# Value products of the sink attention as three rounded products, in one layer of a streaming encoder

## What is computed

```python
s = jnp.einsum("bnqhgd,bnkhd->bnhgqk", q, k) * ATTN_SCALE
s = jnp.where(mask, s, -jnp.inf)
m = jnp.maximum(jnp.max(s, axis=-1, keepdims=True), sink)
e = jnp.exp(s - m)
p = e / (jnp.sum(e, axis=-1, keepdims=True) + jnp.exp(sink - m))
return jnp.einsum("bnhgqk,bnkhd->bnqhgd", p, v)        # the value product
```

## Time and profile before

| | us |
|---|---|
| median of 3 runs (lowest, highest) | 2725.19 (2724.36, 2726.61) |
| the profiled execution: its time | 2727.1 |
| its span, first to last instruction | 2725.5 |
| TensorE busy with matmuls in the span | 2649.0 (97%) |
| VectorE, ScalarE, GpSimd busy | 1814.1, 1267.0, 459.6 |

### The profile page before, as it was taken

How to read it: one execution, slowest core, us unless ns; L and a number is a source line. 1 busy time by engine, 2 the same in 40 slices (tenths; PEclk the granted TensorE clock), 3 DMA queues, 4 the chain that set the end, 5 groups by cost and what they waited for, 6 DMA issues and landing times.

```text
span 2725.5 us, 50555 instructions
## 1 busy us (share of the span) xinstructions
PE 2649.0 (97%) x19461; PEld 2566.0 (94%) x19461; DVE 1814.1 (67%) x2898; ACT 1267.0 (46%) x2367; POOL 459.6 (17%) x726
## 2 busy tenths in 40 slices
PE   7899999999989989999999999899999999999998
PEld 6787899999979989999999999899999999999998
DVE  7754434343464457688888888788888888877632
ACT  5444434433442225566666666554445455525421
POOL 0110012111221111133333333220111010000000
PEclk9999999999999999999999999999999999999999
DMA  4111122222212225355555555875554563422331
GB/s 157 59 47 39 36 86 83 80 76 80 77 43 78 79 72 182 133 187 187 185 190 192 193 189 193 300 264 181 215 215 134 174 215 108 136 88 78 107 100 58
DMA packets 108283, 360.77 MB, mean 132 GB/s; under 512 B 17696, under 2 KB 25760, under 8 KB 107552
## 3 DMA queue, kind: packets, MB, share of 16 engines
q1 hardware_dynamic: 66880, 224.29, 25.4%
q0 software_dynamic: 39568, 132.23, 13.1%
q10 hardware_dynamic: 1616, 1.18, 0.1%
HBM read 282.59 MB, written 75.04 MB: 131 GB/s over the span
## 4 chain that ended last, share of the span: by engine, by line
PE 92%; DVE 3%; DMA 3%; ACT 1%; issue 1%; ACTq 0%; DVEq 0%; POOL 0%; POOLq 0%
PE tile L614 33%; PE misc L696 18%; PE misc L978 16%; PE tile L696 5%; PE tile L978 4%; PE tile L666 4%; PE misc L807 4%; PE misc L614 3%; DMA a_raw<-in_w 2%; PE misc L787 1%; PE misc L709 1%; PE misc L755 1%; PE misc L754 1%; DVE stat L1565 1%; DMA acc<-h_saved_d 0%
## 5 line engine op out<-in xcount | busy, mean ns | idle before, releaser
L614 PE MATMUL tile<-x_hi,w_hi 128*128 128x288 f32 (+1 forms) x2208 | 498.9, 308 | 17.2 <-DVE x_lo L1542 7.9
L614 PE MATMUL tile<-x_hi,w_lo 128*128 128x288 f32 (+1 forms) x2208 | 476.2, 298 | 0.0
L614 PE MATMUL tile<-x_lo,w_hi 128*128 128x288 f32 (+1 forms) x2208 | 475.8, 297 | 0.0
L614 PEld LDWEIGHTS tile<-x_hi,w_hi 128*128 128x128 f32 (+1 forms) x2208 | 352.6, 189 | 44.5 <-issue 36.3
L614 PEld LDWEIGHTS tile<-x_hi,w_lo 128*128 128x128 f32 (+1 forms) x2208 | 356.8, 189 | 1.3
L614 PEld LDWEIGHTS tile<-x_lo,w_hi 128*128 128x128 f32 (+1 forms) x2208 | 356.7, 189 | 1.2
L1017 ACT ACTIVATE a_lo<-a_raw 128x512 fp32r<-128x512 f32 (+1 forms) x420 | 274.0, 656 | 175.7 <-PE misc L978 88.9
L1472 DVE TENSOR_TENSOR w_lo<-w_raw,w_hi 128x1024 fp32r<-128x1024 f32 x170 | 223.7, 1330 | 151.1 <-ACT w_hi L1017 151.0
L696 PE MATMUL misc<-t_hi,a_lo 128*128 128x288 f32 x1008 | 256.0, 294 | 0.0
L1017 ACT ACTIVATE w_hi<-w_raw 128x1024 fp32r<-128x1024 f32 x170 | 177.2, 1052 | 161.9 <-PE tile L614 126.0
L1898 DVE TENSOR_TENSOR a_lo<-a_raw,a_lo 128x512 fp32r<-128x512 f32 x336 | 221.2, 686 | 0.7 <-ACT a_lo L1017 0.7
(11 more groups left out here) (301 smaller groups left out, 5963.4 us busy)
## 6 DMA issues: line engine op xcount, KB each, us to landing
a_raw<-in_w SPq DMA_DIRECT2D x224, 512.0 KB, 4.1
w_raw<-in_w SPq DMA_DIRECT2D x170, 512.0 KB, 3.6
ops_d<-st POOLq DMA_DIRECT2D x280, 144.0 KB, 3.7
ops_d<-hr POOLq DMA_DIRECT2D x112, 144.0 KB, 4.5
x_hi<-ops_d POOLq DMA_DIRECT2D x24, 576.0 KB, 6.9
x_lo<-ops_d POOLq DMA_DIRECT2D x24, 576.0 KB, 10.1
t_hi<-ops_d POOLq DMA_DIRECT2D x24, 576.0 KB, 12.7
a_lo<-ops_d POOLq DMA_DIRECT2D x9, 576.0 KB, 11.5
```

Source lines behind the costliest of these rows:

```text
L614: ins = nc.tensor.matmul(dst[:, h, :], w, x[:, h * HALF:(h + 1) * HALF], start=first and a == 0, stop=last and a == 2)
```

## The change

The value product of the sink pairs becomes three fp32r products. The values are split into `sv` (rounded) and `sv_lo`, with a plane of 128 columns for each head that is zero in the other head's 64; the turned probabilities are split into `s_pt` and `s_pt_lo`, the latter a new VectorE subtraction in every slot from 3 to 12, on which the next transposes and the product wait (`turn_lo`). The weight splits of these tiles move from steps 0 and 8 to steps 1 and 3 (ScalarE) and 2 and 4 (VectorE). Plain float32 matmuls whose result nobody reads are put in the two idle stretches (`fill`). The new buffers take the place of the norm's scratch `st`.

```diff
+ACT_SPLITS, DVE_SPLITS = (1, 3), (2, 4)
...
@@ TensorE
-                    pe.wait_ge(turn_out, lin(g0 + s + 1, i, dg))
+                    pe.wait_ge(turn_lo if kind == "swa" else turn_out, lin(g0 + s + 1, i, dg))
...
-                    pe.wait_ge(turn_out, lin(g0 + s + 2, i, dg))
+                    pe.wait_ge(turn_lo if kind == "swa" else turn_out, lin(g0 + s + 2, i, dg))
...
+                    if kind == "swa":
+                        dst = out_ps[:, 128 * qt:128 * qt + 128] if qt < 4 else scores_ps[:, 512 - SAMPLE:512]
+                        n = 0
+                        for v, p_ in ((sv, s_pt), (sv_lo, s_pt), (sv, s_pt_lo)):
+                            for k, (vt, at) in enumerate(vals):
...
+                                ins = nc.tensor.matmul(dst, v[0:keys, at, head, :], p_[0:keys, s % 2, width * k:width * k + width],
...
+            def fill(count):
+                for k in range(count):
+                    nc.tensor.matmul(tiles_ps[0][:, 0, 0:128], mean_w[:, :], mean_w[:, :], start=True, stop=True)
...
             first_sums()
+            fill(29)
...
             ln_sums(1)
-
+            wait_freed(pe, T_MLP - 2)
+            wait_freed(pe, T_MLP - 1)
+            fill(31)
@@ ScalarE
-            copy(sv[:, 0:4, :], scores_ps[:, 0:512].rearrange("p (a b) -> p a b", a=4)).then_inc(sv_ready, 1)
-            copy(sv[0:64, 4, :], scores_ps[0:64, 512:640]).then_inc(sv_ready, 1)
-            act.wait_ge(sv_ready, 2)
+            for h in range(2):
...
+                copy(sv[:, 0:4, h, own], turned_values[:, :, own]).then_inc(sv_ready, 1)
+                copy(sv[0:64, 4, h, own], scores_ps[0:64, 512 + 64 * h:576 + 64 * h]).then_inc(sv_ready, 1)
+                copy(sv[:, 5, h, own], cv_raw[:, own]).then_inc(sv_ready, 1)
+            act.wait_ge(sv_ready, 6)
+            act.wait_ge(sv_lo_done, 6)
             set_sinks(0)
...
@@ ScalarE and VectorE (DVE_SPLITS there)
             def swa_pair(q, att, i=None, dp=0):
                 for c in range(KT):
-                    if c % 8 == 0:
-                        ahead.upto(U_QA + 2 * q + c // 8 + 2, i, 2 * dp)
                     swa_part(c, att, i, dp)
+                    if c in ACT_SPLITS:
+                        ahead.upto(U_QA + 2 * q + ACT_SPLITS.index(c) + 2, i, 2 * dp)
                     if q == 1:
                         gates(c)
@@ VectorE
+                if kind == "swa" and 3 <= j <= STEPS + 2:
+                    s = j - 3
+                    width = turn_width(kind, step_of(s)[1])
+                    dve.wait_ge(turn_out, lin(g0 + s + 2, i, dg))
+                    V.tensor_tensor(s_pt_lo[:, s % 2, 0:width], turn_ps[:, 0:width], s_pt[:, s % 2, 0:width], ALU.subtract)\
+                        .then_inc(turn_lo, 1)
...
+            dve.wait_ge(sv_ready, 6)
+            for h in range(2):
...
+                V.tensor_tensor(sv_lo[:, 0:4, h, own], turned_values[:, :, own], sv[:, 0:4, h, own], ALU.subtract).then_inc(sv_lo_done, 1)
+                V.tensor_tensor(sv_lo[0:64, 4, h, own], scores_ps[0:64, 512 + 64 * h:576 + 64 * h], sv[0:64, 4, h, own], ALU.subtract)\
+                    .then_inc(sv_lo_done, 1)
+                V.tensor_tensor(sv_lo[:, 5, h, own], cv_raw[:, own], sv[:, 5, h, own], ALU.subtract).then_inc(sv_lo_done, 1)
@@ GpSimd
-            for k, z in enumerate((sk2[64:128, 0, :].bitcast(f32), sk2[0:64, 1, :].bitcast(f32))):
+            for k, z in enumerate((sk2[64:128, 0, :].bitcast(f32), sk2[0:64, 1, :].bitcast(f32),
+                                   sv[:, :, 0, 64:128].bitcast(f32), sv[:, :, 1, 0:64].bitcast(f32))):
...
             pool.wait_ge(x_ready, 2 + KT)
+            for k, z in enumerate((sv_lo[:, :, 0, 64:128].bitcast(f32), sv_lo[:, :, 1, 0:64].bitcast(f32))):
+                P.memset(z, 0.0).then_inc(zeroed_p, 1)
```

More of the change, by code:

```diff
@@ L252, in build @@
         swa = ExitStack()
-        win_r = sb("win_r", [128, 256], f32r, swa)
         sinks = sb("sinks", [128, 2 * PAIRS], f32, swa)
@@ L257, in build @@
         sq1 = sb("sq1", [128, 2, TOK], f32r, swa)
-        sv = sb("sv", [128, 6, 128], f32, swa)
+        sv = sb("sv", [128, 6, 2, 128], f32r, swa)
+        cv_raw = sb("cv_raw", [128, 128], f32, swa)
         s_p = sb("s_p", [128, 4, 2 * 128 + 1], f32, swa)
-        s_pt = sb("s_pt", [128, 2, 256], f32, swa)
         cos_t = sb("cos_t", [128, TOK], f32, swa)
@@ L309, in build @@
         staged = (st[:, 0, :], st[:, 1, :])
+        st_flat = st_r[:, :, :].rearrange("p a b -> p (a b)")
+        sv_lo = st_flat[:, 0:1536].rearrange("p (a h b) -> p a h b", a=6, h=2)
+        s_pt = st_flat[:, 1536:2048].rearrange("p (a b) -> p a b", a=2)
+        s_pt_lo = st_flat[:, 2048:2560].rearrange("p (a b) -> p a b", a=2)
+        win_r = st_flat[:, 2560:2816]
         ops_d = nc.dram_tensor("ops_d", (JOBS, 2, FAST, 128, HALF), f32, kind="Internal").ap()
@@ L348, in build @@
         op_act, op_dve, op_pool = sem("op_act"), sem("op_dve"), sem("op_pool")
-        va_ready, va_turned, sv_ready = sem("va_ready"), sem("va_turned"), sem("sv_ready")
+        va_turned, sv_ready = sem("va_turned"), sem("sv_ready")
         kv_out = sem("kv_out")
@@ L361, in build @@
         turn_out = sem("turn_out")
+        turn_lo, sv_lo_done = sem("turn_lo"), sem("sv_lo_done")
         weighed = sem("weighed")
         out_free = sem("out_free")
-        v_ready, v_turned, fv_ready = sem("v_ready"), sem("v_turned"), sem("fv_ready")
-        k_ready = sem("k_ready")
+        v_turned, fv_ready = sem("v_turned"), sem("fv_ready")
         v_out, k_out, forget_rows = sem("v_out"), sem("k_out"), sem("forget_rows")
@@ L383, in build @@
         y_sum, y_ready = sem("y_sum"), sem("y_ready")
-        p_landed, p_hi_done, p_ready, pe_ready = sem("p_landed"), sem("p_hi_done"), sem("p_ready"), sem("pe_ready")
-        gate, gated = sem("gate"), sem("gated")
+        p_landed, p_hi_done, p_ready = sem("p_landed"), sem("p_hi_done"), sem("p_ready")
+        gated = sem("gated")
         y_out = [sem("y_out0"), sem("y_out1")]
-        ch_act, ch_dve, ch_pool = sem("ch_act"), sem("ch_dve"), sem("ch_pool")
+        ch_dve, ch_pool = sem("ch_dve"), sem("ch_pool")
         OP_KV = 4
@@ L491, in build @@
         block = outer.enter_context(nc.Block())
-        ZERO_SWA, ZERO_ALL = 2, 2 + 6
+        ZERO_SWA, ZERO_ALL = 6, 6 + 6
         f_tmp = acc[0:16, :, :].rearrange("p k t -> p (k t)")
@@ L782, in attend @@
                     pe.wait_ge(normed, lin(g0 + s + 1, i, dg))
-                    pe.wait_ge(turn_out, lin(g0 + s + 1, i, dg))
+                    pe.wait_ge(turn_lo if kind == "swa" else turn_out, lin(g0 + s + 1, i, dg))
+                    if kind == "fox" and pair == PAIRS and s == 0:
+                        pe.wait_ge(turn_lo, STEPS * PAIRS + 1)
                     cols_ = key_cols(kind, head, qt)
@@ L804, in attend @@
                     vals = value_tiles(kind, qt)
+                    if kind == "swa":
[3 more added lines that the diff above has]
+                            for k, (vt, at) in enumerate(vals):
+                                keys = SAMPLE if qt == 4 and k == len(vals) - 1 else 128
+                                n += 1
+                                ins = nc.tensor.matmul(dst, v[0:keys, at, head, :], p_[0:keys, s % 2, width * k:width * k + width],
+                                                       start=s in (0, 8) and n == 1, stop=n == 3 * len(vals),
+                                                       skip_group_check=s not in (0, 8))
+                        ins.then_inc(weighed, 1)
+                        return
                     for k, (vt, at) in enumerate(vals):
@@ L864, in swa_keys_ready @@
                 pe.wait_ge(zeroed_p, ZERO_SWA)
-                pe.wait_ge(sv_ready, 2)
+                pe.wait_ge(sv_ready, 6)
+                pe.wait_ge(sv_lo_done, 6)
                 pe.wait_ge(masks, 3)
@@ L1100, in _ @@
                 act.dma_start(dst[:, :], t[name]).then_inc(consts, 16)
-            act.dma_start(sv[:, 5, :], t["swa_cv"]).then_inc(consts, 16)
+            act.dma_start(cv_raw[:, :], t["swa_cv"]).then_inc(consts, 16)
             for c in range(KT):
@@ L1128, in _ @@
             act.wait_ge(va_turned, 1)
-            copy(sv[:, 0:4, :], scores_ps[:, 0:512].rearrange("p (a b) -> p a b", a=4)).then_inc(sv_ready, 1)
-            copy(sv[0:64, 4, :], scores_ps[0:64, 512:640]).then_inc(sv_ready, 1)
-            act.wait_ge(sv_ready, 2)
+            act.wait_ge(zeroed_p, 4)
+            for h in range(2):
+                own = slice(64 * h, 64 * h + 64)
+                turned_values = scores_ps[:, 0:512].rearrange("p (a b) -> p a b", a=4)
+                copy(sv[:, 0:4, h, own], turned_values[:, :, own]).then_inc(sv_ready, 1)
[3 more added lines that the diff above has]
+            act.wait_ge(sv_lo_done, 6)
             set_sinks(0)
@@ L1195, in fox_pair @@
                 for c in range(3 * KT):
-                    if c % 8 == 0 and q is not None:
```

(13 more changed lines are left out.)

## The result

The changed kernel takes 2746.7 us (median of 4 runs, 2744.9 to 2749.5) against 2725.1 on the same chip: a ratio of 1.0079, 95% interval 1.0062 to 1.0097. It is slower by 21.6 us. The forecast was slower by 10, and its upper bound was 2744: the sign was right, the size was not. The profiled execution took 2746.5 with a span of 2744.9, 19.4 more than the one of before.

A forecast was written before the change was run, and what follows sets the result against it. TensorE was taken to bound the kernel (92% of the chain). First pair +9.0, pairs 1 to 6 +3.0, clock +3.0, pair 7 -2.3 and fills -2.65 gave +10.0: 2735 us median, range 2720 to 2744 (forecast's own 2729 to 2742).

The forecast's parts named there:

- the first pair: First sink pair: later rotation +0.9, two splits +2.3, gates' stretch +2.4, tail +3.4; sum +9.0 us, bounds 6 and 13.
- pairs 1 to 6: Each: value product -1.0, old stalls -1.54, slot waits +1.04, last subtraction +2.0; +0.5, together +3.0 us; clock falls +3.0 more.
- pair 7: Last sink pair, no rotation behind it: -1.0 - 1.54 + 1.04 + 0.7 (split at step 16) - 1.5 = -2.3 us.
- value product's term: TensorE's value product: six fp32r matmuls in 0.66 us against 0.68 plain, plus edge savings; -1.0 a pair, bounds 0 and -1.6.
- The wait for the last subtraction: Step 9's value product waits for VectorE's slot 12 low half, behind `rotate` and `lows`: 2.0 us in all pairs but the last.
- The clock: TensorE's granted clock falls in five of six pairs in place of three, at 1.5 us a fall: +3.0 us.
- The fills: Fills before both quads keep the clock up: -1.55 and -1.1 us, 0.31 a fill, bounds together -3.5 and +3.0.
- (a): Last low half is not late: seven waits of 2.0 and five to six clock falls go, 2713 us; chance 0.13.
- (b): The new wait at the value product does not lower the clock: five falls (7.5 us) go, 2727.5; chance 0.18.
- (c): The slot chain binds: 0.3 us more for signals in six slots of seven pairs, +12.6, 2748 us; chance 0.10.
- (d): Fills run at 0.40 us or the clock falls anyway: +3.0 for -2.65, 2741 us; chance 0.07.
- (e): Weight loads hide, an fp32r matmul of 128 tokens taking 0.08 us: -0.8 in seven pairs, 2729.5; chance 0.05.

The follow-up runs named there:

- padded rows: Changed kernel with the sample queries' second key tile padded from 64 to 128 key rows by zero rows: 2733.7 us (1.0031).
- both corrections: Changed kernel with sample-step key rows padded to 128 and each pair's last VectorE subtraction put ahead of the rotation's low halves: 2713.2 us (0.9955).
- the plain product and the moved splits: Kernel before the change with the moved weight splits and the fills, keeping the plain value product: 2704.8 us (0.9922).
- the moved subtraction: Changed kernel with VectorE's last subtraction of a pair between the rotation and its low halves, not behind them: 2728.8 us (1.0013).
- the kernel grouped by row count: Changed kernel with a sample step's three 128-row products first, then its three 64-row ones: 2737.0 us (1.0044).

## Why the forecast was right in sign and half in size

**The step that failed** is in the value product: that the two steps with sample queries "lose a little, since 64 tokens do not shorten a load", 0.66 a step. A step takes 1.35, 0.225 a matmul: where the row count changes from one weight load to the next, the second begins only when the first has ended (two loads of 0.19 in 0.41), and where it stays it begins 0.11 after the first began. With equal rows the step takes 0.69, near the forecast. I had looked at what 64 tokens cost and not at the row count of the second key tile, which stands in the code I costed. It is worth 1.3 to 1.4 a pair in TensorE's work. With this step alone put right, by the padded rows, the kernel takes 2733.7 against a forecast of 2735, and its profile goes with the forecast place by place: the tail of the first pair +3.6 (forecast 3.4), pairs 1 to 6 +4.7 (6.0) with five falls of the clock (five), pair 7 -2.6 (-2.3).

The rest of the value product's term was too hopeful as well: with both corrections TensorE's own work is 26.85 - 0.52 = 26.33 a pair against 26.88 - 0.19 = 26.69 with the plain product and the moved splits, a gain of 0.36 and not of 1.0; from the transposes to the column products a full slot takes 0.84 to 0.87 where it took 0.89. That the forecast comes out with padded rows is so in part luck: this shortfall is made up by smaller waits (0.52 and 1.66 where 1.04 and 2.0 were forecast).

**The wait for the last subtraction** was right in place, cause and number of times. It is 0.97 and not 2.0 because TensorE comes there 4.60 after the swap (3.72 forecast), late from the slow step ahead of it, while the product may start 5.55 after it (5.68 forecast). With that step mended the wait is 1.66.

**The clock** fell in all of the pairs 1 to 6 (five of six forecast). The wait is enough to bring a fall, as forecast: with equal rows and the wait, five of six show one. What the forecast did not have is that the slow steps are enough too: without the wait three of six still fall, and with neither none does.

**Pairs 1 to 6** by these numbers: own work +1.02, old stalls -1.54, slot 4 +0.52, value product +0.96, together +0.96 a pair, and three falls more at 1.5: 5.8 + 4.5 = 10.3; measured 10.4, forecast 6.0. The own work is what is left of a pair of 31.0 when its waits and its fall are taken off, so this sum has to close; but the padded kernel's pair without a fall gives it as well: 28.85 - 0.52 - 1.66 = 26.67, and 1.3 for two slow steps, 28.0 against 26.98 before. The forecast had the same terms, and the slot waits at half their forecast 1.04 helped.

**The first pair**: up to the first maximum +3.0, of which about 1 is this execution's (the six kernels of the experiments with the same splits and subtractions up to there start at 113.0 to 113.9, this one at 114.73); the other 2 stand against a forecast of 1.65. The gates' stretch grew by 2.9 (forecast 2.4), the tail by 5.7 (3.4); with padded rows, where the granted clock in the tail is 1.00 in place of 0.88, by 3.6: the slow steps and the lowered clock are the difference. For the two splits the forecast had +2.3, less about 1 for the one that no longer stands ahead; putting them back with both corrections is worth the 1.3 that are left (113.03 to 111.74), though starts of the same code differ by 0.9, and with the plain product the move cost nothing.

**Pair 7** lost 1.0 where -2.3 was forecast: its own two slow steps (1.4) and a longer fall behind them. The wait at its sample transposes (L797, 0.64) is the 0.7 of the forecast. With padded rows it gains 2.6.

**The fills** gained more than forecast, -1.6 and -1.9 for -1.55 and -1.1: 29 of them take 6.64, so a fill is under 0.23, below the low bound of 0.24, and the overrun that I took off does not exist.

**The rivals.** (a) fell: the low half is late. (b) fell: the clock does fall behind the wait. (c) did not come: the later pairs' slots wait in one place only. (d) fell: the quads start at the higher clock. (e) fell: 0.11 a matmul, not 0.08.

## What to carry to other kernels

Cost a stream of small matmuls by the rows, columns and tokens of each neighbour, not of each matmul alone: two shapes that alternate can cost twice what either costs (here 0.225 for 0.11). When a change bundles parts, price each by itself: here the splits alone give 18.5 us and the fills 3.5, and the new product, as it was written, costs 42 on top of the two (2704.8 to 2746.7). Where an engine's order puts a small result behind long work that waits for someone else, look for that idle time ahead of the long work first: the moved subtraction cost nothing and gave 18.

## What the runs showed of the hardware that I had not expected

Matmuls with 128 weight columns and 64 tokens start 0.11 to 0.13 apart when their row counts are equal (128 or 64), and 0.225 apart when 128 and 64 rows alternate. The profile shows the loads too. In the changed kernel two take 0.41, one behind the other. In the kernel grouped by row count, single loads of 0.19 start 0.11 apart, for 128 rows as for 64, and only the two where the count changes take 0.41:

```profile
240.76 0.41 PEld L819 LDWEIGHTS misc<-st_r,sv 128*128 128x128 f32 x2
```

```profile
236.28 0.19 PEld L821 LDWEIGHTS misc<-st_r,sv 128*128 128x128 f32 x1
236.39 0.19 PEld L821 LDWEIGHTS misc<-st_r 128*128 128x128 f32 x1
236.50 0.41 PEld L821 LDWEIGHTS misc<-st_r,sv 128*128 128x128 f32 x2
236.84 0.19 PEld L821 LDWEIGHTS misc<-st_r 64*128 64x128 f32 x1
236.95 0.19 PEld L821 LDWEIGHTS misc<-st_r,sv 64*128 64x128 f32 x1
```

The Trainium skill, "TensorE: Matmul & The Clock Gate", section "Step-by-step: what each phase is for", says that a load is pulled ahead of a running matmul where the row groups do not conflict or where it goes to the background buffer for weights, and that the row count does not matter to a load's time. The trace agrees with the second half, 0.19 for a load of either row count; what the alternation costs lies between two loads. Whether the first half is the reason no run here shows.

The granted clock can fall from 2.4 to 1.2 GHz while the profile shows TensorE busy without a gap, behind the two steps of such alternating matmuls: it does in three of six pairs of the kernel with the moved subtraction (its windows above), and in none when the rows are made equal and the rest stays.
